# First FFN chunks of a decoder layer by rows of blocks, with h taken from PSUM and filler products in front

## The chip, the core and the metric

The kernel runs on one core of a Trainium2 chip. The core has TensorE (PE: matrix products and transposes, results in PSUM), VectorE (DVE), ScalarE (ACT), GpSimd (POOL), and SyncE (SP), which issues nearly all the loads. The metric is the device time of one execution in microseconds (us).

## What is computed

One layer of a hybrid decoder, 512 tokens of width 1024, all in f32:

```python
h = rms_norm(x, ffn1_norm)
x = x + 0.5 * (silu(h @ w_gate) * (h @ w_up)) @ w_down     # D_FF = 2816
# then: pooling and sliding-window attention with w_in and w_out,
# a second FFN of the same form, and x + sigmoid(rms_norm(x) @ w_g) * (p @ w_p)
```

The change touches only the beginning: loading x and the first weights, turning x so that features lie on partitions, multiplying it by the gains, and the first products of the first FFN.

## The kernel before

**Precision.** Each f32 operand is split into a high part in fp32r (written by ScalarE as a rounding copy) and a low part, the remainder (VectorE for activations, POOL for weights). A product is then three products of TensorE: high x high, low x high, high x low (`product`, lines 1112 to 1116). Weights come in chunks of 128 x 1024 f32 (512 KB) into a ring of four slots: `raw` (as loaded), `w_hi`, `w_lo`. For gate and up, one chunk is one block of 128 output features over all eight blocks k of input features, in the order gate 0, up 0, gate 1, up 1, and so on. `w_hi_done`, `w_ready` (low part done) and `w_used` (products done) count chunks.

**The norm.** h is not divided by the root of the mean square before the products. `h_hi` and `h_lo` are x times the gain; the statistic is made beside the products: ScalarE squares x block by block (`h_square`), VectorE adds the squares into `sumsq` (`h_add`), and one product with a tile of ones, `stat`, sums over the partitions. `rstd_of` on ScalarE makes the inverse root by Ln and Exp. VectorE applies it to the products' results.

**The opening.** SP loads x in four parts of 256 columns, in turn with the first four chunks, then p and eleven small gain vectors. PE turns x block by block into banks 4 to 7 (`turn_x`, four transposes a block). VectorE copies each to `x_t`; ScalarE makes `h_hi` from `x_t`, VectorE `h_lo`. PE multiplies pair by pair of blocks k, for the first two chunks (slots 0 and 1) into banks 0 and 1. Then it turns the gains and p, and does slots 2 and 3 in one go, with `stat` in the middle of slot 2. Each engine's order is written out by hand, with semaphores as the only link; an engine never passes over a waiting instruction.

**The loop.** `ffn_tensor` then goes through the chunks in groups of four, eight blocks each. It waits for the chunk's `w_ready` and for VectorE to have read the bank. On ScalarE `ffn_scalar` comes after `rstd_of(0, 4)`: its first action is the split of chunk 4 (line 468), which waits for the load and for slot 0 to be used. POOL's `lo_of` follows it. The load of chunk 4 itself waits on SP until slot 0's low part is made (`put`).

## Time and profile before

| | us |
|---|---|
| median of 3 runs | 938.45 |
| lowest, highest | 937.75, 938.58 |
| profiled execution | 938.35 |
| its span, first to last instruction | 936.6 |
| PE busy | 923.4 (99%) |
| PE weight loads busy | 759.6 (81%) |
| DVE, ACT, POOL busy | 297.9, 385.3, 414.0 |

A row of the order of time gives start, duration, engine, line of the kernel, operation, what it writes and reads, how many instructions are merged, and in brackets how long the engine had been idle and what ended that. Products overlap: a product's duration is longer than the distance to the next one's start, so paces are read from starts.

### The profile page before, as it was taken

The numbers are of one execution on the slowest core, as the hardware profiler recorded it, in microseconds if no ns is written. First come the engines' busy times: TensorE is split into PE (matmuls) and PEld (weight loads), VectorE is DVE, ScalarE is ACT, GpSimd is POOL, SyncE is SP. The second block draws the span as 40 slices with busy tenths as digits, with TensorE's granted clock in tenths as the row PEclk, the third lists the DMA queues.
The fourth block names the chain that finished last, engine by engine and source line by source line (L and its number), as shares of the span: only waits on it lengthen the run. The fifth ranks groups of instructions, "written<-read, shape, count | busy, mean of one in ns | idle before, by whom it ended". The sixth has DMA issues, their size and how long they took to land.

```text
span 936.6 us, 11393 instructions
## 1 busy us (share of the span) xinstructions
PE 923.4 (99%) x4104; PEld 759.6 (81%) x4104; DVE 297.9 (32%) x467; ACT 385.3 (41%) x514; POOL 414.0 (44%) x191
## 2 busy tenths in 40 slices
PE   7999999999999999999999999999999999999998
PEld 5888888888888888777788788888888888888886
DVE  6511122211100501659978532111112200410532
ACT  5734444433321421565844644433444321321641
POOL 3554444444444444345645354444444444444340
PEclk9999999999999999999999999999999999999999
DMA  8333333332332333231223143333333323332221
GB/s 251 108 113 99 102 90 94 108 90 90 107 95 90 90 112 90 60 99 34 68 68 113 54 126 103 99 90 94 107 90 91 108 93 90 99 103 90 74 73 56
DMA packets 129650, 89.25 MB, mean 95 GB/s; under 512 B 11312, under 2 KB 114776, under 8 KB 129624
## 3 DMA queue, kind: packets, MB, share of 16 engines
q1 hardware_dynamic: 129608, 88.90, 31.9%
q8 instruction: 16, 0.26, 0.1%
q14 instruction: 10, 0.08, 0.0%
q10 hardware_dynamic: 16, 0.00, 0.0%
HBM read 86.80 MB, written 2.10 MB: 95 GB/s over the span
## 4 chain that ended last, share of the span: by engine, by line
PE 94%; DVE 4%; issue 1%; DMA 0%; ACT 0%; DVEq 0%; ACTq 0%
PE bank L1114 31%; PE bank L1115 31%; PE bank L1116 31%; PE bank L1129 1%; DVE sumsq L745 1%; DVE h_lo L736 1%; DVE probs L923 1%; PE bank L1260 0%; DMA x_nat<-in_x 0%; PE bank L1134 0%; DVE x_t L1088 0%; DVE tmp L1087 0%; DVE pr_lo L949 0%; DVE small L931 0%; ACT h_hi L428 0%
## 5 line engine op out<-in xcount | busy, mean ns | idle before, releaser
L324 POOL TENSOR_TENSOR w_lo<-raw,w_hi 128x1024 fp32r<-128x1024 f32 x161 | 390.2, 2426 | 479.1 <-ACT w_hi L468 240.4
L1114 PE MATMUL bank<-h_hi,w_hi 128*128 128x512 f32 x848 | 335.2, 395 | 0.3 <-DVE h_lo L736 0.3
L1115 PE MATMUL bank<-h_lo,w_hi 128*128 128x512 f32 x848 | 330.7, 390 | 0.0
L1116 PE MATMUL bank<-h_hi,w_lo 128*128 128x512 f32 x848 | 330.6, 390 | 0.0
L1114 PEld LDWEIGHTS bank<-h_hi,w_hi 128*128 128x128 f32 x848 | 159.6, 188 | 36.8 <-issue 2.3
L1115 PEld LDWEIGHTS bank<-h_lo,w_hi 128*128 128x128 f32 x848 | 159.7, 188 | 34.5 <-issue 1.9
L1116 PEld LDWEIGHTS bank<-h_hi,w_lo 128*128 128x128 f32 x848 | 159.6, 188 | 33.2
L419 ACT ACTIVATE w_hi<-raw 128x1024 fp32r<-128x1024 f32 x81 | 85.7, 1060 | 223.3 <-PE bank L1116 218.6
L468 ACT ACTIVATE w_hi<-raw 128x1024 fp32r<-128x1024 f32 x80 | 84.4, 1060 | 190.9 <-PE bank L1116 190.9
L1114 PE MATMUL bank<-act_hi,w_hi 128*128 (+1 forms) x352 | 136.9, 389 | 0.0
L1115 PE MATMUL bank<-act_lo,w_hi 128*128 (+1 forms) x352 | 136.9, 389 | 0.0
L1116 PE MATMUL bank<-act_hi,w_lo 128*128 (+1 forms) x352 | 136.9, 389 | 0.0
L762 DVE TENSOR_TENSOR tmp<-bank,tmp 128x512 f32<-128x512 f32 x44 | 30.4, 692 | 285.9 <-ACT tmp L456 285.9
L1116 PEld LDWEIGHTS bank<-act_hi,w_lo 128*128 128x128 f32 x352 | 66.1, 188 | 13.8
L1114 PEld LDWEIGHTS bank<-act_hi,w_hi 128*128 128x128 f32 x352 | 66.1, 188 | 13.7
L1115 PEld LDWEIGHTS bank<-act_lo,w_hi 128*128 128x128 f32 x352 | 66.1, 188 | 13.6
L785 DVE SCALAR_TENSOR_TENSOR tmp<-bank,rstd 128x512 f32<-128x512 f32 x16 | 11.1, 692 | 197.1 <-PE bank L1116 196.7
L764 DVE TENSOR_TENSOR act_lo<-tmp,act_hi 128x512 f32 (+1 forms) x44 | 38.2, 869 | 39.5 <-ACT act_hi L458 39.5
L458 ACT ACTIVATE act_hi<-tmp 128x512 f32 (+1 forms) x44 | 27.8, 633 | 37.4 <-DVE tmp L762 37.4
L759 DVE TENSOR_TENSOR tmp<-bank,rstd 128x512 f32<-128x512 f32 x44 | 30.4, 690 | 36.7 <-PE bank L1116 30.7
L456 ACT ACTIVATE tmp<-tmp 128x512 f32<-128x512 f32 x44 | 27.4, 623 | 0.2
L736 DVE SCALAR_TENSOR_TENSOR h_lo<-x_t,gain,h_hi 128x512 fp32r<-128x512 f32 x32 | 26.2, 856 | 3.0 <-ACT h_hi L428 2.7
(149 smaller groups left out, 621.5 us busy)
## 6 DMA issues: line engine op xcount, KB each, us to landing
raw<-in_ffn_w_gate SPq DMA_DIRECT2D x44, 512.0 KB, 3.7
raw<-in_ffn_w_up SPq DMA_DIRECT2D x44, 512.0 KB, 3.7
raw<-in_ffn_w_down SPq DMA_DIRECT2D x44, 512.0 KB, 3.7
raw<-in_w_ple_gate SPq DMA_DIRECT2D x8, 512.0 KB, 3.7
raw<-in_w_in SPq DMA_DIRECT2D x6, 512.0 KB, 3.7
x_nat<-in_x SPq DMA_DIRECT2D x4, 512.0 KB, 7.0
raw<-in_w_in SPq DMA_DIRECT2D x8, 256.0 KB, 3.2
raw<-in_w_out SPq DMA_DIRECT2D x4, 512.0 KB, 3.4
```

What stands on the lines that cost most here:

```text
L324: pool.tensor_tensor(w_lo[:, slot, :], raw[:, slot, :], f32(w_hi[:, slot, :]), ALU.subtract).then_inc(w_ready, 1)
L419: nc.scalar.activation(w_hi[:, slot, :], raw[:, slot, :], ACT.Copy).then_inc(w_hi_done, 1)
L456: nc.scalar.activation(tmp[:, 2 * (f % 2), :], tmp[:, 2 * (f % 2), :], ACT.Silu).then_inc(silu_done, 1)
L458: nc.scalar.activation(act_hi[:, f + 2 * quad, :], tmp[:, 2 * (f % 2) + 1, :], ACT.Copy).then_inc(act_hi_done, 1)
L468: nc.scalar.activation(w_hi[:, slot, :], raw[:, slot, :], ACT.Copy).then_inc(w_hi_done, 1)
L736: nc.vector.scalar_tensor_tensor(h_lo[:, d, :], x_t[:, d, :], gain[:, ph * KD + d:ph * KD + d + 1], f32(h_hi[:, d, :]), ALU.mult, ALU.subt ...
L759: nc.vector.tensor_tensor(a, gb[:], rstd[:], ALU.mult).then_inc(gate_scaled, 1)
L762: nc.vector.tensor_tensor(t, ub[:], a, ALU.mult).then_inc(act_made, 1)
L764: nc.vector.tensor_tensor(act_lo[:, f + 2 * quad, :], t, f32(act_hi[:, f + 2 * quad, :]), ALU.subtract).then_inc(act_ready, 1)
L1114: nc.tensor.matmul(dst, a_hi, b_hi, start=first, stop=False)
L1115: nc.tensor.matmul(dst, a_hi, b_lo, start=False, stop=False)
L1116: return nc.tensor.matmul(dst, a_lo, b_hi, start=False, stop=last)
```

## The change

- **Loads.** x comes in five parts (blocks 0, 1, 2-3, 4-5, 6-7, from the list `FIRST`). Behind each part come the same rows of blocks of all four first chunks: for each block k one load of gate and one of up, each filling two slots.
- **Splits.** ScalarE's splits and POOL's low parts of the first four chunks go by the same parts, over all four slots at once. VectorE makes the low part of row 0 itself.
- **h from PSUM.** ScalarE's rounding and VectorE's remainder read the turned x from PSUM, in banks 4 to 6 in turn; the copy to `x_t` comes after them.
- **Products.** For each block k PE does all four slots (12 products), with turns of x in between. Blocks 6 and 7 come last, slot by slot, after the turns of gains and p; `stat` stands behind slot 0's last rows.
- **Filler.** Seven products of the tile of ones with itself into bank 3, which nobody reads, stand ahead of the first turns. The turn of the first gains moves ahead of those of x.
- The loads' counts for later chunks are shifted to fit, and `w_ready` of the first four chunks now rises by four at once, with the last part.

```diff
@@ -50,11 +50,13 @@
     CHUNKS = PLE + KD
     TWO_PART = {C_Q, C_Q + 1, C_Q + 2, C_Q3} | {C_WA + i for i in range(HALF)}
     QUADS = NF // 2
+    WARM = 7
+    FIRST = ((0, 1), (1, 2), (2, 4), (4, 6), (6, 8))
 
     def loads_of(slot, c0, quad=0):
 
         extra = sum(1 for c in TWO_PART if c <= c0 and c % SLOTS == slot)
-        return 16 * (c0 // SLOTS + 1 + extra) + 16 * quad
+        return 16 * (c0 // SLOTS + extra) + 16 * quad
 
     es = ExitStack()
     with es:
...
@@ -230,19 +234,26 @@
 
 
             x_v = x[0].rearrange("(b p) c -> p b c", p=P)
-            W = D // 4
-
-            def load_x(i):
-                sp.dma_start(x_nat[:, :, i * W:(i + 1) * W], x_v[:, :, i * W:(i + 1) * W]).then_inc(x_loaded[i], 16)
-
-            load_x(0)
-            gate_up(0, ffn1_w_gate, 0)
-            load_x(1)
-            gate_up(1, ffn1_w_up, 0)
-            load_x(2)
-            load_x(3)
-            gate_up(2, ffn1_w_gate, 1)
-            gate_up(3, ffn1_w_up, 1)
+            def load_x(eng, s):
+                k0, k1 = FIRST[s]
+                eng.dma_start(x_nat[:, :, k0 * P:k1 * P], x_v[:, :, k0 * P:k1 * P]).then_inc(x_loaded[s], 16)
+
+            def load_first(s):
+
+                k0, k1 = FIRST[s]
+                for j, w in enumerate((ffn1_w_gate, ffn1_w_up)):
+                    for k in range(k0, k1):
+                        sp.dma_start(raw[:, j:SLOTS:2, k * P:(k + 1) * P],
+                                     w[0, k * P:(k + 1) * P, 0:2 * P].rearrange("p (f c) -> p f c", f=2))\
+                            .then_inc(first_loaded[s], 16)
+
+            load_x(sp, 0)
+            load_first(0)
+            load_x(sp, 1)
+            load_first(1)
+            for s in range(2, len(FIRST)):
+                load_x(sp, s)
+                load_first(s)
             sp.dma_start(p_nat[:], p[0, 0].rearrange("(b p) c -> p b c", p=P)).then_inc(p_loaded, 16)
 
             rows = KD
@@ -324,8 +335,17 @@
                 pool.tensor_tensor(w_lo[:, slot, :], raw[:, slot, :], f32(w_hi[:, slot, :]),
                                    ALU.subtract).then_inc(w_ready, 1)
 
-            for c in range(SLOTS):
-                lo_of(c, c + 1)
+            for s in range(1, len(FIRST)):
+                cols = slice(FIRST[s][0] * P, FIRST[s][1] * P)
+                if s < len(FIRST) - 1:
+                    pool.wait_ge(first_hi_done, s + 1)
+                else:
+                    pool.wait_ge(w_hi_done, SLOTS)
+                ins = pool.tensor_tensor(w_lo[:, :, cols], raw[:, :, cols], f32(w_hi[:, :, cols]), ALU.subtract)
+                if s < len(FIRST) - 1:
+                    ins.then_inc(first_lo_done, 1)
+                else:
+                    ins.then_inc(w_ready, SLOTS)
             with pool.Fori(1, (C_K + 2) // SLOTS) as quad:
                 for slot in range(SLOTS):
                     lo_of(slot, quad * SLOTS + slot + 1)
...
@@ -492,30 +512,46 @@
 
             act.dma_start(gain_nat[0:KD, :], ffn1_norm[0].rearrange("(k p) -> k p", p=P)).then_inc(gain1_loaded, 16)
 
-            split(0)
+            def first_split(s):
+                cols = slice(FIRST[s][0] * P, FIRST[s][1] * P)
+                act.wait_ge(first_loaded[s], 32 * (FIRST[s][1] - FIRST[s][0]))
+                ins = nc.scalar.activation(w_hi[:, :, cols], raw[:, :, cols], ACT.Copy)
+                if s < len(FIRST) - 1:
+                    ins.then_inc(first_hi_done, 1)
+                else:
+                    ins.then_inc(w_hi_done, SLOTS)
+
+            def first_round(d):
+                act.wait_ge(x_turned, d + 1)
+                nc.scalar.activation(h_hi[:, d, :], bank[4 + d % 3][:], ACT.Copy,
+                                     scale=gain[:, d:d + 1]).then_inc(h_hi_done, 1)
+
+            first_split(0)
             act.wait_ge(gain1_ready, 1)
-            h_round(0, 0)
-            h_round(0, 1)
-            split(1)
+            first_round(0)
+            first_split(1)
+            first_round(1)
             h_square(0, 0)
+            first_split(2)
+            first_round(2)
             h_square(0, 1)
-            h_round(0, 2)
-            h_round(0, 3)
+            first_split(3)
+            first_round(3)
             h_square(0, 2)
+            first_split(4)
+            first_round(4)
             h_square(0, 3)
-            h_round(0, 4)
-            h_round(0, 5)
-            split(2)
-            h_round(0, 6)
-            h_round(0, 7)
-            split(3)
-            for d in range(HALF, KD):
-                h_square(0, d)
+            first_round(5)
+            h_square(0, 4)
+            first_round(6)
+            h_square(0, 5)
+            first_round(7)
+            h_square(0, 6)
+            h_square(0, 7)
             for k in range(2):
                 act.wait_ge(p_turned, k + 1)
-                nc.scalar.activation(pt_hi[:, k, :], bank[5 + k][:], ACT.Copy).then_inc(p_hi_done, 1)
-            rstd_of(0, 4)
-            act.wait_ge(gain_ready, 3)
+                nc.scalar.activation(pt_hi[:, k, :], bank[6 - 2 * k][:], ACT.Copy).then_inc(p_hi_done, 1)
+            rstd_of(0, 5)
             ffn_scalar(0, FFN1)
             for d in range(HALF, KD):
                 h_square(1, d)
@@ -819,25 +855,47 @@
                                       sink_in[:].rearrange("p (g t) -> p g t", g=2)).then_inc(gain_ready, 1)
 
 
-            for pair in range(HALF):
-                for d in (2 * pair, 2 * pair + 1):
-                    dve.wait_ge(x_turned, d + 1)
-                    nc.vector.tensor_copy(x_t[:, d, :], bank[4 + d % 4][:]).then_inc(x_ready, 1)
-                dve.wait_ge(x_ready, 2 * pair + 2)
-                if pair == 0:
-                    dve.wait_ge(gain_turned, 1)
-                    nc.vector.tensor_copy(gain[:, 0:KD], bank[7][:, 0:KD]).then_inc(gain1_ready, 1)
-                    dve.wait_ge(gain1_ready, 1)
-                h_rest(0, 2 * pair)
-                h_rest(0, 2 * pair + 1)
-                if pair == 1:
-                    h_add(0, 1)
-            for d in range(2, KD):
-                h_add(0, d)
+            def first_rest(d):
+                dve.wait_ge(h_hi_done, d + 1)
+                nc.vector.scalar_tensor_tensor(h_lo[:, d, :], bank[4 + d % 3][:], gain[:, d:d + 1],
+                                               f32(h_hi[:, d, :]), ALU.mult, ALU.subtract).then_inc(h_ready, 1)
+
+            def first_copy(d):
+                nc.vector.tensor_copy(x_t[:, d, :], bank[4 + d % 3][:]).then_inc(x_ready, 1)
+
+            dve.wait_ge(gain_turned, 1)
+            nc.vector.tensor_copy(gain[:, 0:KD], bank[7][:, 0:KD]).then_inc(gain1_ready, 1)
+            dve.wait_ge(gain1_ready, 1)
+            first_rest(0)
+            dve.wait_ge(first_hi_done, 1)
+            nc.vector.tensor_tensor(w_lo[:, :, 0:P], raw[:, :, 0:P], f32(w_hi[:, :, 0:P]),
+                                    ALU.subtract).then_inc(first_lo_dve, 1)
+            first_copy(0)
+            first_rest(1)
+            first_copy(1)
+            first_rest(2)
+            first_copy(2)
+            h_add(0, 1)
+            first_rest(3)
+            first_copy(3)
+            h_add(0, 2)
+            first_rest(4)
+            first_copy(4)
+            h_add(0, 3)
+            first_rest(5)
+            first_copy(5)
+            h_add(0, 4)
+            first_rest(6)
+            first_copy(6)
+            h_add(0, 5)
+            first_rest(7)
+            first_copy(7)
+            h_add(0, 6)
+            h_add(0, 7)
             later_gains()
             for k in range(2):
                 dve.wait_ge(p_hi_done, k + 1)
-                nc.vector.tensor_tensor(pt_lo[:, k, :], bank[5 + k][:], f32(pt_hi[:, k, :]), ALU.subtract)\
+                nc.vector.tensor_tensor(pt_lo[:, k, :], bank[6 - 2 * k][:], f32(pt_hi[:, k, :]), ALU.subtract)\
                     .then_inc(p_ready, 1)
             dve.wait_ge(gain_ready, 3)
             ffn_vector(0, FFN1)
...
@@ -1197,49 +1255,64 @@
 
             def turn_x(d):
 
-                if d % 2 == 0:
-                    pe.wait_ge(x_loaded[d // 2], 16)
-                if d == 3:
-                    pe.wait_ge(gain1_ready, 1)
-                if d >= 4:
-                    pe.wait_ge(x_ready, d - 3)
+                for s in range(len(FIRST)):
+                    if d == FIRST[s][0]:
+                        pe.wait_ge(x_loaded[s], 16)
+                if d >= 3:
+                    pe.wait_ge(x_ready, d - 2)
                 for b in range(NB):
-                    ins = turn(bank[4 + d % 4][:, b * P:(b + 1) * P], x_nat[:, b, d * P:(d + 1) * P])
+                    ins = turn(bank[4 + d % 3][:, b * P:(b + 1) * P], x_nat[:, b, d * P:(d + 1) * P])
                 ins.then_inc(x_turned, 1)
 
+            def first_ready(k):
+
+                pe.wait_ge(h_ready, k + 1)
+                if k == 0:
+                    pe.wait_ge(first_lo_dve, 1)
+                elif k < FIRST[4][0]:
+                    pe.wait_ge(first_lo_done, 1 if k < 2 else k // 2 + 1)
+                else:
+                    pe.wait_ge(w_ready, SLOTS)
+
+            def first_step(k):
+                first_ready(k)
+                for j in range(SLOTS):
+                    from_h(bank[j][:], j, k, k + 1)
+
+            pe.wait_ge(dve_consts, 1)
+            for i in range(WARM):
+                nc.tensor.matmul(bank[3][:, 0:P], ones[:], ones[:], start=True, stop=True)
+            pe.wait_ge(gain1_loaded, 16)
+            turn(bank[7][:, 0:KD], gain_nat[0:KD, :], KD).then_inc(gain_turned, 1)
             turn_x(0)
             turn_x(1)
-            pe.wait_ge(gain1_loaded, 16)
-            turn(bank[7][:, 0:KD], gain_nat[0:KD, :], KD).then_inc(gain_turned, 1)
+            first_step(0)
             turn_x(2)
+            first_step(1)
             turn_x(3)
-
-            for pair in range(HALF):
-                pe.wait_ge(h_ready, 2 * pair + 2)
-                for j in range(2):
-                    if pair == 0:
-                        pe.wait_ge(w_ready, j + 1)
-                    ins = from_h(bank[j][:], j, 2 * pair, 2 * pair + 2)
-                    if pair == HALF - 1:
-                        ins.then_inc(w_used, 1)
-                if pair < 2:
-                    turn_x(4 + 2 * pair)
-                    turn_x(5 + 2 * pair)
+            first_step(2)
+            turn_x(4)
+            first_step(3)
+            turn_x(5)
+            turn_x(6)
+            first_step(4)
+            turn_x(7)
+            first_step(5)
             pe.wait_ge(gains_loaded, 16 * 11)
-            pe.wait_ge(x_ready, KD)
             turn(bank[7][:, 0:GAINS], gain_nat[:], GAINS).then_inc(gain_turned, 1)
             pe.wait_ge(p_loaded, 16)
             for k in range(2):
+                pe.wait_ge(x_ready, KD - 2 + k)
                 for b in range(NB):
-                    ins = turn(bank[5 + k][:, b * P:(b + 1) * P], p_nat[:, b, k * P:(k + 1) * P])
+                    ins = turn(bank[6 - 2 * k][:, b * P:(b + 1) * P], p_nat[:, b, k * P:(k + 1) * P])
                 ins.then_inc(p_turned, 1)
-            for j in range(2, SLOTS):
-                pe.wait_ge(w_ready, j + 1)
-                from_h(bank[j][:], j, 0, HALF)
-                if j == 2:
+            first_ready(KD - 2)
+            first_ready(KD - 1)
+            for j in range(SLOTS):
+                from_h(bank[j][:], j, KD - 2, KD).then_inc(w_used, 1)
+                if j == 0:
                     pe.wait_ge(dve_consts, 4 + PAD)
-                    stat(0, 4)
-                from_h(bank[j][:], j, HALF, KD).then_inc(w_used, 1)
+                    stat(0, 5)
             ffn_tensor(0, FFN1)
 
 
```

## Rows read from the trace of the kernel before

**Rows 1.** The page: busy time of each engine; the slices of PE.

```profile
PE 923.4 (99%) x4104; PEld 759.6 (81%) x4104; DVE 297.9 (32%) x467; ACT 385.3 (41%) x514; POOL 414.0 (44%) x191
...
PE   7999999999999999999999999999999999999998
```

**Rows 2.** Order of time to 15 us: start, duration, engine, line, operation, idle before.

```profile
1.19 0.29 POOL L319 TENSOR_SCALAR_AFFINE_SELECT ident<-ident 128x128 f32<-128x128 f32 x1 [0.24 <-POOL ident L317]
...
4.31 1.94 PE L1129 MATMUL bank<-ident,x_nat 128*128 128x128 f32 x8 [4.31 <-DMA x_nat<-in_x]
5.51 1.47 DVE L825 COPY x_t<-bank 128x512 f32<-128x512 f32 x2 [3.57 <-PE bank L1129]
5.92 1.06 ACT L419 ACTIVATE w_hi<-raw 128x1024 fp32r<-128x1024 f32 x1 [3.23 <-DMA raw<-in_ffn_w_gate]
...
7.21 1.34 ACT L428 ACTIVATE h_hi<-x_t,gain 128x512 fp32r<-128x512 f32 x2 [0.24 <-DVE gain L829]
8.04 2.58 DVE L736 SCALAR_TENSOR_TENSOR h_lo<-x_t,gain,h_hi 128x512 fp32r<-128x512 f32 x2 [0.86 <-ACT h_hi L428]
...
14.55 0.68 DVE L745 TENSOR_TENSOR sumsq<-sumsq,tmp 128x512 f32<-128x512 f32 x1
```

**Rows 3.** Order of time on PE, 10 to 15 us: the first products.

```profile
10.67 0.79 PE L1114 MATMUL bank<-h_hi,w_hi 128*128 128x512 f32 x1 [0.29 <-DVE h_lo L736]
...
11.69 0.63 PE L1116 MATMUL bank<-h_hi,w_lo 128*128 128x512 f32 x1
12.12 0.63 PE L1114 MATMUL bank<-h_hi,w_hi 128*128 128x512 f32 x1
...
14.43 0.39 PE L1116 MATMUL bank<-h_hi,w_lo 128*128 128x512 f32 x1
14.65 0.39 PE L1114 MATMUL bank<-h_hi,w_hi 128*128 128x512 f32 x1
```

**Rows 4.** Busy time by stretch; last three columns: granted clock, DMA share, GB/s.

```profile
12.00:14.00 2.00, 2.00 (x5) 1.18 (x5) 1.30 (x2) 1.73 (x3) 1.41 (x1) 1.00 1.15 338
...
16.00:18.00 2.00, 2.00 (x12) 1.72 (x11) 1.73 (x3) 1.29 (x3) 0.00 (x0) 1.00 0.07 21
```

**Rows 5.** Order of time on PE: products on either side of transposes.

```profile
15.12 0.40 PE L1116 MATMUL bank<-h_hi,w_lo 128*128 128x512 f32 x1
...
16.46 0.40 PE L1115 MATMUL bank<-h_lo,w_hi 128*128 128x512 f32 x1
...
25.38 0.39 PE L1116 MATMUL bank<-h_hi,w_lo 128*128 128x512 f32 x1
...
27.05 0.39 PE L1115 MATMUL bank<-h_lo,w_hi 128*128 128x512 f32 x1
```

**Rows 6.** Order of time, 29 to 39 us, PE, ACT, POOL: statistic to loop.

```profile
29.57 1.02 PE L1134 MATMUL bank<-sumsq,ones 128*128 128x512 f32 x2
...
38.63 0.39 PE L1114 MATMUL bank<-h_hi,w_hi 128*128 128x512 f32 x1
...
30.70 0.69 ACT L444 ACTIVATE rstd<-bank,scalars 128x512 f32<-128x512 f32 x1
31.40 1.28 ACT L446 ACT_TABLE_LOAD   x1
33.35 1.28 ACT L468 ACT_TABLE_LOAD   x1
34.64 2.01 ACT L468 ACTIVATE w_hi<-raw 128x1024 fp32r<-128x1024 f32 x2
...
35.78 4.76 POOL L324 TENSOR_TENSOR w_lo<-raw,w_hi 128x1024 fp32r<-128x1024 f32 x2 [10.24 <-ACT w_hi L468]
```

**Rows 7.** Order of time on PE and POOL around FFN2's statistic.

```profile
526.48 1.12 PE L1134 MATMUL bank<-sumsq,ones 128*128 128x512 f32 x2 [0.81 <-DVE sumsq L745]
...
531.45 4.77 POOL L324 TENSOR_TENSOR w_lo<-raw,w_hi 128x1024 fp32r<-128x1024 f32 x2 [15.56 <-ACT w_hi L468]
```

**Rows 8.** The chain that ended last, at the statistic: start, us, what.

```profile
29.73 0.86 PE bank L1134 x2
```

More of the change, by code:

```diff
@@ L123, in layer @@
         bank = [es.enter_context(nc.psum_tensor(f"bank{i}", [P, S], F32)) for i in range(8)]
-        x_loaded = [sem(f"x_loaded{i}") for i in range(4)]
+        x_loaded = [sem(f"x_loaded{i}") for i in range(len(FIRST))]
+        first_loaded = [sem(f"first_loaded{i}") for i in range(len(FIRST))]
+        first_hi_done, first_lo_dve, first_lo_done = sem("first_hi_done"), sem("first_lo_dve"), sem("first_lo_done")
         p_loaded, gains_loaded, sinks_loaded = sem("p_loaded"), sem("gains_loaded"), sem("sinks_loaded")
```

## The prediction

> **What bounds the kernel now.** I read the page first. TensorE (PE) is busy for 923.4 of the 936.6 us of span [rows 1], so the time is PE's work plus the 13 us in which it has none, and an edit pays only where it changes those 13 us or the pace of the products. Then I read the order of time of the first 40 us, since the diff touches nothing behind them. PE starts at 4.31 with transposes of x, its first product starts at 10.67, and the first product of the loop over FFN chunks (chunk 4) at 38.63 [rows 2, 3, 6]. From there PE goes on without a gap, one product each 0.2275 us. So the change is worth what it moves the start at 38.63, and nothing else counts. I call that start the loop start. The 96 products of the opening cost 96 x 0.2275 = 21.8 us of the 38.63, whatever their order.
>
> The third thing to see is the pace: until about 14 us products start 0.43 us apart (11.69 to 12.12), later 0.22 apart (14.43 to 14.65) [rows 3]. That is the lower and the upper of PE's two levels, 1.2 and 2.4 GHz, although the granted clock in the row of that stretch reads 1.00 [rows 4]; here only the pitch tells the level. Eight products ran at the lower one, which cost 8 x 0.2 = 1.6 us.
>
> The fourth is what runs up to the loop start. The opening's statistic (ones times the sum of squares) starts on PE at 29.57. ScalarE then has in a row: Ln at 30.70, a table load at 31.40, Exp, a table load at 33.35, and only then the two splits at 34.64, the first of which is chunk 4; POOL makes its low part from 35.78, two in 4.76 us, so chunk 4 is ready at 38.16 [rows 6]. From statistic to ready chunk: 8.6 us. PE covers this with 36 products (8.2 us) and the statistic itself (0.86), 9.06 us, and arrives 0.45 us after the chunk. A wait of nearly nine microseconds is hidden with half a microsecond to spare. FFN2 has the same chain with one table load less: statistic at 526.48, POOL from 531.45, ready at 533.84, 7.4 us = 8.6 less 1.28 [rows 7]. So I trust 8.6.
>
> **The change, part by part.**
>
> *The first product.* The seven filler products can start when the identity is made (1.19 + 0.29 = 1.48, POOL) [rows 2]; an f32 product of 512 columns takes 0.86 at the upper level [rows 8], so one of 128 columns 0.215, or 0.43 at the lower: 7 x 0.43 = 3.0, and PE is free at 4.55. That is 0.25 later than its start on x now. The turn of the gains takes 0.2, so x's first block starts at 4.75. VectorE saw the first turned block 1.20 after its start (5.51 against 4.31), and from ScalarE's rounding to VectorE's remainder it was 0.83 (7.21 to 8.04) [rows 2]: rounding at 5.95, first_rest at 6.8. The copy to x_t no longer stands in between; that is what "straight from PSUM" saves. first_rest takes 0.7 (the add at 14.55 took 0.68 with POOL idle) to 1.3 (two remainders in 2.58 beside POOL); take 0.75. Then VectorE makes w_lo of row 0, 0.7 to 1.3, its first part before POOL has its own work. First product at 8.5, between 8.2 and 9.1, against 10.67: 2.2 us earlier. The loads don't set it: the gate load of 512 KB, which has the 512 KB of x ahead of it, let ScalarE start at 5.92, and in the new order x's first block and its weights are 512 KB together, so they are there by about 4.5.
>
> *From there to the statistic.* Now 60 products and 16 transposes of x lie between the first product and the statistic; then 78 products and 24 transposes. 78 x 0.2275 = 17.75. Eight transposes between products cost 1.34 - 2 x 0.2275 = 0.885 (15.12 to 16.46) and the turns of gains and p 1.67 - 0.455 = 1.215 (25.38 to 27.05) [rows 5], so 3 x 0.885 + 1.215 = 3.9. Sum 21.6. The same sum for the kernel now (10.67 + 13.65 + 1.77 + 1.215 + 1.6 for the low clock = 28.9) is 0.66 short of 29.57, some of it a wait for the second chunk's low part; I carry 0.3, since row blocks are ready sooner. The statistic starts at 8.5 + 21.6 + 0.3 = 30.4, which is 0.8 *later* than now: it now stands behind 78 products instead of 60.
>
> *Is PE fed in between?* One row of blocks is 12 products and a turn, 2.73 + 0.44 = 3.2 us. VectorE needs for it a remainder, a copy (two in 1.47) and an add (0.68), 2.1 us, and up to 3 beside POOL [rows 2]; ScalarE a rounding, a square and half a split of 1.06, 1.8; POOL 1.2. The loads run at 338 GB/s until after 14 us and are over in 16 to 18 [rows 4], so all 4 MB of x and first weights are there at about 14, and the last split and its low part by about 20, while the last two rows are wanted at 29. The tightest are row 2's low part (13.5 against 14.9) and the last add (29.4 against 30.4). I cost these at nothing; if the cover goes, VectorE's last two adds put up to 1 us before the statistic. SP issues 16 weight loads in place of four, about 0.5 us each, in time while the engines are saturated. The reload of all four slots now waits for the last low part (20) instead of slot by slot (17.5); it takes 4 us and is wanted at 33: nothing.
>
> *From the statistic to the loop.* This part of ScalarE's order is untouched: rstd, then the split of chunk 4. But the statistic now stands behind slot 0's last rows, and only slots 1 to 3's last rows, 18 products (4.1 us), follow it. PE is through at 30.4 + 0.86 + 4.1 = 35.4 and chunk 4 is ready at 30.4 + 8.6 = 39.0, plus 0.05. So PE stands idle for 3.7 us in front of the loop, a wait that doesn't exist now. What follows is covered: the next chunk comes 2.4 us later and PE works 5.4 us on each. Loop start at 39.05 against 38.63: 0.4 us later. The 3.3 us by which PE is through earlier, 38.63 to 35.4, go into the wait.
>
> *The clock.* No row shows what the filler does to the level. From below: it is at the upper level by the first product, and nothing is to be added. From above: it is no better than now, eight products at the lower, 1.6 us. PE is then busy from 1.55 to 6.3 almost without a break, where it now is for 4.31 to 6.3; I lean to the lower end and take 0.4. The Trainium skill, "TensorE: Matmul & The Clock Gate", section "What's actually happening", says that the idle array is the throttled one and that sustained work releases it; the rows agree, the pitch halves after dense products.
>
> Sum: 38.63 becomes 39.05 + 0.4 = 39.45, +0.8 us. The profiled execution took 938.35 with a span of 936.6, the runs' median is 938.45. 938.35 + 0.8 = 939.2.
>
> **The rivals.**
>
> 1. *The clock falls in the new idle time.* PE has no gap of this length once it runs, so no row shows what follows one. What the start shows is the price of the lower level: some eight products, 1.6 us. 939.2 + 1.6 = 940.8, slower than before. It decides once the wait for chunk 4 is long enough for the level to drop. For it: 3.7 us without work is over four times the gap in rows 7. Against it: the gap of 0.81 in front of FFN2's statistic [rows 7] cost nothing behind it. The same page of the Trainium skill, section "Why this matters for your kernels", warns that a long idle gap between bursts takes the array back to half rate; that rule speaks for this rival, and no run shown bears on it. Chance 0.14.
> 2. *The filler does not raise the clock.* Then the lower level lasts as now until 12 to 14 us, from 8.5 on: up to 13 products x 0.2 = 2.6 in place of 0.4, about 941.0. For it: the transposes of 4.31 to 6.3 and 8.41 to 10 did not raise it. Against: the filler more than doubles the unbroken stretch. Chance 0.12.
> 3. *The wait for chunk 4 does not come about.* If its split did not stand behind rstd, the loop would start at 35.4 and the time would be 935.1. Against it is the whole chain in rows 6 and 7. Chance 0.04.
> 4. *The filler works at once.* The level is up by the first turns, those take half, the first product comes at 8.0, the statistic at 29.7, the loop at 38.3: 938.0. Chance 0.08.
> 5. *Small loads are slow.* 21 issues in place of eight, each with its own start and end. The second kind of weights waits for row 4 only from 21 us on, so it decides only if the stream takes over 5 us longer; then about 942. The Trainium skill, "DMA: Bandwidth & Descriptors", section "Rules for kernel authors", speaks against the change in wanting few, large transfers; by it the loads run longer, which the slack above would take up. Chance 0.04.
>
> **How the numbers follow.** Forecast as summed 0.58, the rivals 0.14, 0.12, 0.04, 0.08, 0.04. A measurement of this kernel can tell about 0.2%, 1.9 us, from no change: 936.6 to 940.3. Faster is rival 3: 0.04. Slower are rivals 1, 2 and 5, less their mild ends, 0.26. Within is the forecast and rival 4 with those ends: 0.70. The range leaves out rival 3 and the worst of 1, 2 and 5: 937.5 to 941.3.
>
> **What would show it.** First product near 8.5; turns of x interleaved with groups of 12 products; the statistic near 30.4; PE idle for 3.7 us with the release "POOL w_lo" in front of the loop's first product, at about 39; the same three table loads. If PE's idle time there is under 2 us, my chain is wrong. If products behind the gap start 0.43 apart, rival 1 is right; if those up to 12 us do, rival 2. If VectorE's sumsq releases the statistic, the adds were not covered.

## The result

The changed kernel takes 943.0 us, median of 6 runs (941.56 to 943.19), against 938.56 for the kernel before: ratio 1.0043, 95% interval 1.0033 to 1.0054. It is slower by 4.4 us, 0.4%. The forecast was 939.2 with a range up to 941.3; the time lies outside it, and on the side that I gave 0.26.

| | before | after |
|---|---|---|
| profiled execution, its span | 938.35, 936.6 | 943.06, 941.3 |
| first product | 10.67 | 8.53 |
| products at the lower level at the start | 8 | 12 |
| statistic | 29.57 | 33.11 |
| PE idle in front of the loop | 0 | 3.48 |
| loop start | 38.63 | 41.72 |
| products at the lower level behind it | 0 | 7 to 8 |

Order of time on PE in the kernel after, the same view as [rows 2, 3].

```profile
1.53 3.36 PE L1284 MATMUL bank<-ones 128*128 128x128 f32 x14 [1.53 <-DVE head_ones L838]
4.82 0.27 PE L1187 MATMUL bank<-ident,gain_nat 8*128 8x8 f32 x1
5.02 1.11 PE L1187 MATMUL bank<-ident,x_nat 128*128 128x128 f32 x4
6.45 1.11 PE L1187 MATMUL bank<-ident,x_nat 128*128 128x128 f32 x4 [0.31 <-DMA x_nat<-in_x]
8.53 0.77 PE L1172 MATMUL bank<-h_hi,w_hi 128*128 128x512 f32 x1 [0.97 <-DVE w_lo L871]
...
13.36 0.63 PE L1174 MATMUL bank<-h_hi,w_lo 128*128 128x512 f32 x1
13.79 0.87 PE L1187 MATMUL bank<-ident,x_nat 128*128 128x128 f32 x4
14.41 0.47 PE L1172 MATMUL bank<-h_hi,w_hi 128*128 128x512 f32 x1
14.72 0.39 PE L1173 MATMUL bank<-h_lo,w_hi 128*128 128x512 f32 x1
```

The filler runs, the first product comes 2.1 us earlier than before, and the 12 products of row 0 take from 8.53 to 13.79, 5.26 us; at the upper level they would take 2.73. In this execution the filler had not raised the level when the first product came.

From the statistic to the loop, first PE, then ScalarE and POOL, the same view as [rows 6].

```profile
33.11 1.02 PE L1192 MATMUL bank<-sumsq,ones 128*128 128x512 f32 x2
...
37.86 0.39 PE L1174 MATMUL bank<-h_hi,w_lo 128*128 128x512 f32 x1
41.72 0.79 PE L1172 MATMUL bank<-h_hi,w_hi 128*128 128x512 f32 x1 [3.48 <-POOL w_lo L335]
42.31 0.63 PE L1173 MATMUL bank<-h_lo,w_hi 128*128 128x512 f32 x1
42.74 0.63 PE L1174 MATMUL bank<-h_hi,w_lo 128*128 128x512 f32 x1
...
34.16 0.69 ACT L464 ACTIVATE rstd<-bank,scalars 128x512 f32<-128x512 f32 x1 [0.30 <-PE bank L1192]
34.87 1.28 ACT L466 ACT_TABLE_LOAD   x1
...
36.82 1.28 ACT L488 ACT_TABLE_LOAD   x1
38.11 2.00 ACT L488 ACTIVATE w_hi<-raw 128x1024 fp32r<-128x1024 f32 x2
...
39.24 4.67 POOL L335 TENSOR_TENSOR w_lo<-raw,w_hi 128x1024 fp32r<-128x1024 f32 x2 [16.43 <-ACT w_hi L488]
```

Statistic at 33.11, chunk 4 ready at 39.24 + 2.34 = 41.58: 8.5 us, as forecast. PE is through at 38.1 and stands still until POOL releases it. Behind the gap products start 0.43 apart. Busy time by stretch of the kernel after (granted clock, DMA share and GB/s last) now shows the lower level itself: 0.50.

```profile
38.00:40.00 2.00, 0.25 (x2) 0.00 (x0) 0.00 (x0) 1.99 (x3) 0.76 (x1) 1.00 0.00 0
40.00:42.00 2.00, 0.28 (x1) 0.28 (x2) 0.00 (x0) 1.97 (x3) 2.00 (x2) 0.91 0.00 0
42.00:44.00 2.00, 2.00 (x5) 1.54 (x6) 1.05 (x2) 1.08 (x3) 1.92 (x1) 0.50 0.42 120
44.00:46.00 2.00, 2.00 (x8) 1.62 (x7) 1.06 (x2) 2.00 (x3) 1.37 (x1) 0.74 0.82 237
```

The account closes: the loop starts 3.1 us later (41.72 against 38.63), and eight products then take 3.47 us (41.72 to 45.19) in place of 1.82, 1.65 more. Together 4.7, which is the difference of the spans.

### The profile page after: what moved, and what is told of

Read it like the earlier page. It is cut to its first block, busy times and chain, and to the rows that moved or that the text cites. A ratio compares the mean times of both kernels' runs of the same rounds, so it can differ in the third digit from the quotient of the medians.

```text
span 941.3 us, 11441 instructions
## 1 busy us (share of the span) xinstructions
PE 928.3 (99%) x4118; PEld 763.9 (81%) x4118; DVE 294.0 (31%) x468; ACT 385.4 (41%) x515; POOL 413.0 (44%) x191
## 4 chain that ended last, share of the span: by engine, by line
PE 92%; DVE 4%; issue 3%; ACT 1%; DMA 0%; POOL 0%; SPq 0%; DVEq 0%; POOLq 0%; ACTq 0%
PE bank L1172 30%; PE bank L1174 30%; PE bank L1173 30%; PE bank L1187 1%; DVE sumsq L781 1%; DVE probs L981 1%; PE bank L1333 0%; DMA raw<-in_ffn_w_up 0%; DVE x_t L1146 0%; DVE tmp L1145 0%; DVE pr_lo L1007 0%; POOL w_lo L335 0%; DVE h_lo L772 0%; DVE small L989 0%; PE bank L1192 0%
## 5 line engine op out<-in xcount | busy, mean ns | idle before, releaser
L335 POOL TENSOR_TENSOR w_lo<-raw,w_hi 128x1024 fp32r<-128x1024 f32 x157 | 380.1, 2424 | 472.6 <-ACT w_hi L488 248.0
L439 ACT ACTIVATE w_hi<-raw 128x1024 fp32r<-128x1024 f32 x77 | 81.5, 1061 | 218.7 <-PE bank L1174 218.6
L488 ACT ACTIVATE w_hi<-raw 128x1024 fp32r<-128x1024 f32 x80 | 84.4, 1060 | 192.2 <-PE bank L1174 192.0
L798 DVE TENSOR_TENSOR tmp<-bank,tmp 128x512 f32<-128x512 f32 x44 | 30.4, 692 | 287.6 <-ACT tmp L476 287.6
L1172 PEld LDWEIGHTS bank<-act_hi,w_hi 128*128 128x128 f32 x352 | 66.1, 188 | 13.8
L800 DVE TENSOR_TENSOR act_lo<-tmp,act_hi 128x512 f32 (+1 forms) x44 | 38.1, 866 | 39.5 <-ACT act_hi L478 39.5
L795 DVE TENSOR_TENSOR tmp<-bank,rstd 128x512 f32<-128x512 f32 x44 | 30.4, 690 | 37.4 <-PE bank L1174 33.9
```

The lines of the kernel that those rows point to most:

```text
L335: pool.tensor_tensor(w_lo[:, slot, :], raw[:, slot, :], f32(w_hi[:, slot, :]), ALU.subtract).then_inc(w_ready, 1)
L439: nc.scalar.activation(w_hi[:, slot, :], raw[:, slot, :], ACT.Copy).then_inc(w_hi_done, 1)
L488: nc.scalar.activation(w_hi[:, slot, :], raw[:, slot, :], ACT.Copy).then_inc(w_hi_done, 1)
L795: nc.vector.tensor_tensor(a, gb[:], rstd[:], ALU.mult).then_inc(gate_scaled, 1)
L798: nc.vector.tensor_tensor(t, ub[:], a, ALU.mult).then_inc(act_made, 1)
L800: nc.vector.tensor_tensor(act_lo[:, f + 2 * quad, :], t, f32(act_hi[:, f + 2 * quad, :]), ALU.subtract).then_inc(act_ready, 1)
```

## The experiments

Two questions: is the wait in front of the loop, with the fall of the clock behind it, one separable cost with one cause (the statistic's place)? And why did the filler bring nothing: is it useless for the level, or is its effect lost before the first product? All times are medians beside the kernel before on the same chip, whose medians were 938.7 to 938.8.

| run | median (lowest to highest) | ratio to before, 95% |
|---|---|---|
| e1_no_filler | 943.36 (943.13 to 943.72) | 1.0049 (1.0035 to 1.0063) |
| e2_filler16 | 945.28 (944.84 to 945.95) | 1.0069 (1.0055 to 1.0083) |
| e3_no_wait | 936.33 (935.21 to 937.97) | 0.9974 (0.9963 to 0.9984) |
| e4_gap_filled | 941.16 (939.05 to 941.85) | 1.0024 (1.0015 to 1.0033) |
| e5_tables_only | 941.86 (937.58 to 942.06) | 1.0019 (1.0008 to 1.0031) |
| e6_no_wait_no_filler | 937.15 (936.52 to 937.82) | 0.9980 (0.9971 to 0.9989) |
| e7_no_wait_holes | 935.17 (935.01 to 935.74) | 0.9960 (0.9947 to 0.9974) |
| e8_late_stat | 944.55 (944.35 to 946.07) | 1.0063 (1.0051 to 1.0076) |
| e9_round_first | 935.21 (934.95 to 935.43) | 0.9963 (0.9950 to 0.9977) |
| e10_before_filled | 938.06 (937.62 to 940.41) | 0.9997 (0.9988 to 1.0006) |
| e11_after_holes | 940.38 (939.04 to 940.63) | 1.0014 (1.0005 to 1.0023) |

### The wait: e8_late_stat, e3_no_wait, e4_gap_filled, e5_tables_only

**e8_late_stat**, the kernel before with the statistic moved:

```diff
-                from_h(bank[j][:], j, 0, HALF)
-                if j == 2:
+                from_h(bank[j][:], j, 0, 2)
+                if j == 3:
                     pe.wait_ge(dve_consts, 4 + PAD)
                     stat(0, 4)
-                from_h(bank[j][:], j, HALF, KD).then_inc(w_used, 1)
+                from_h(bank[j][:], j, 2, KD).then_inc(w_used, 1)
```

> The kernel before, with nothing changed but the place of the statistic: six products into slot 3, so that 18 products stand between it and the loop in place of 36. Theory A (the wait in front of the loop comes from this place alone): PE gets to the statistic 18 products (4.1 us) later, chunk 4 is ready 8.6 us after it, a gap of 3.6 us opens in front of the loop and the level falls behind it: 938.6 + 3.6 + 1.5 to 3.0, 943.7 to 945.2. Rival F (the wait of the changed kernel comes from the loads by rows or from all four slots being freed together): no gap here, 938.6.

Measured 944.55, as theory A put it. The first products of e8's loop on PE:

```profile
42.97 0.79 PE L1114 MATMUL bank<-h_hi,w_hi 128*128 128x512 f32 x1 [3.49 <-POOL w_lo L324]
43.56 0.63 PE L1115 MATMUL bank<-h_lo,w_hi 128*128 128x512 f32 x1
```

The kernel before has no loads by rows, no shared release of slots and no filler, and gets the same gap (3.49 against 3.48 us) with slow products behind it, from one moved instruction. The place of the statistic is enough to cause both. Of the 6.0 us by which e8's profiled execution is longer than that of the kernel before, 3.5 are the gap and 1.7 the slow products; most of the rest is a statistic 0.7 us later than the move alone makes it, behind a first product at 11.10 in place of 10.67 and products at the lower level until 15.6.

**e3_no_wait**, the changed kernel with ScalarE's order mended; the loop's first round of splits is written out and the loop begins at 2:

```diff
+            act.preload_act_table_set("natural_log_exp_and_others")
             first_split(0)
...
+            split(SLOTS)
             rstd_of(0, 5)
             ffn_scalar(0, FFN1)
```

> The changed kernel with ScalarE's order mended: the split of chunk 4 stands ahead of the inverse root (the loop's first round of splits is written out for this), and the table that holds copy, square, Ln and Exp is loaded at the start, so no load stands between. Chunk 4 is then ready 3.6 us after the statistic begins and PE arrives after 5.0. Theory A (the wait costs 3.5 us and the drop of the level behind it 1.5 us, nothing else): PE goes into the loop without a gap at 38.1, at 0.23 us pitch, and the time is 943.0 - 3.6 - 1.5 = 937.9. Rival B (something else bounds that place, the read of bank 0 or the loads): a gap of over 1 us stays and the time is 940 or more.

Measured 936.33. ScalarE of e3, where the split of chunk 4 stands first and no table load is left before it or between Ln and Exp:

```profile
31.89 1.06 ACT L439 ACTIVATE w_hi<-raw 128x1024 fp32r<-128x1024 f32 x1 [0.81 <-PE bank L1182]
32.85 0.67 ACT L464 ACTIVATE rstd<-bank,scalars 128x512 f32<-128x512 f32 x1
33.55 0.63 ACT L466 ACTIVATE rstd<-rstd 128x512 f32<-128x512 f32 x1
```

PE goes into the loop without a gap. The same opening is now 2.4 us faster than before instead of 4.4 slower. It gained 6.7, 1.6 more than forecast: in its profiled execution the level also rose earlier at the start (at 11.4 in place of 13.8), which is the matter of the next section. e4, whose code up to the loop is that of the changed kernel, had an earlier rise as well (12.2), so it comes without e3's edit; what sets it in an execution stays open.

**e4_gap_filled**, fifteen unread products of h between the statistic's tail and the loop:

```diff
+            pe.wait_ge(gain_ready, 1)
+            for i in range(15):
+                nc.tensor.matmul(bank[7][:], h_hi[:, 0, 0:P], h_hi[:, 0, :], start=True, stop=True)
             ffn_tensor(0, FFN1)
```

> The changed kernel with fifteen unread products of h (512 columns, 0.2275 us each, 3.4 us) in PE's idle time in front of the loop. The wait for chunk 4 stays as it is. Theory A (the 3.5 us without work let the level fall, which cost seven products x 0.2 us): the loop starts at the same 41.7 us, but at 0.23 us pitch at once, and the time falls by 1.5 us to 941.5. Rival B (the level fell for another reason, or falls by chance): the first seven products of the loop stay 0.43 us apart and the time stays at 943.

Measured 941.16. The wait is kept, only PE is busy in it, and the loop starts at the upper level:

```profile
40.59 0.49 PE L1172 MATMUL bank<-h_hi,w_hi 128*128 128x512 f32 x1
40.92 0.39 PE L1173 MATMUL bank<-h_lo,w_hi 128*128 128x512 f32 x1
```

So the fall comes from the idle time. Its price, read from the eight slow products of the changed kernel, is some 1.6 us. The median is lower by 1.8; the profiled execution also had the earlier rise at the start, so the median alone does not give the price.

**e5_tables_only**, of e3 the line with the table alone.

> The changed kernel with one line added: ScalarE loads the table that holds copy, square, Ln and Exp at the start, so the two loads of 1.28 us between the statistic and the split of chunk 4 go; their order stays. Theory A (the wait is the chain's length less PE's cover, and the level falls only behind a long idle time): chunk 4 is ready 6.0 us after the statistic begins, PE waits 1.1 us in place of 3.5 and goes on at 0.23 us pitch; time 936.3 (no wait at all) + 1.1 = 937.4. Rival C (any wait in front of the loop drops the level): 1.1 us of wait and seven or more products 0.43 apart, 939 to 940.

Measured 941.86, far off both the 937.4 and most of the gain. Two things were wrong in my expectation. First, only the load before Exp went; the one at the loop's entry stayed (35.76 in ScalarE's row below), so the wait is 2.20 us and not 1.1. Second, the level fell here too, but late: the first five products behind the gap ran fast, those from 42.0 on slow. e5 on ScalarE, on PE, and by stretch:

```profile
35.76 1.28 ACT L488 ACT_TABLE_LOAD   x1
...
40.68 0.49 PE L1173 MATMUL bank<-h_hi,w_hi 128*128 128x512 f32 x1 [2.20 <-POOL w_lo L335]
41.01 0.39 PE L1174 MATMUL bank<-h_lo,w_hi 128*128 128x512 f32 x1
...
41.99 0.63 PE L1175 MATMUL bank<-h_hi,w_lo 128*128 128x512 f32 x1
42.41 0.63 PE L1173 MATMUL bank<-h_hi,w_hi 128*128 128x512 f32 x1
42.84 0.63 PE L1174 MATMUL bank<-h_lo,w_hi 128*128 128x512 f32 x1
```

```profile
42.00:44.00 2.00, 2.00 (x6) 1.63 (x5) 1.41 (x2) 2.00 (x3) 1.30 (x2) 0.50 0.90 256
```

Two of its twelve runs took 937.6, 4.3 below the median. That would fit executions in which neither the start nor the gap met the lower level (some 12 + 8 products x 0.2 us), but only one execution has a trace, so this stays open.

### The filler: e1, e2, e6, e7, e11, e10, e9

**e1_no_filler** sets `WARM = 0`, **e2_filler16** `WARM = 16`.

> The changed kernel without its seven filler products. Theory A (the filler never reached the clock: in the changed kernel products run 0.43 us apart until 13.8, as long as before): the level rises at about the same time, 14 us; the first block of x is turned at 4.3 in place of 5.0, the first product comes up to 0.6 us earlier, at 8.0, and the time falls by 0 to 0.5 us from 943.0. Rival B (the filler did its part and without it the level would rise later still): the rise moves from 14 to 15 or later and the time rises by 0.5 to 1.5 us.

> Sixteen filler products in place of seven, so PE is busy without a break from 1.5 to about 9.2 us (16 x 2 x 0.24 = 7.7). Theory A (this kind of filler, f32 over 128 columns, does not raise the level at all): first product at about 12.7 to 13, at the lower level, the level rises 3 to 5 us after it, time 943 + 4 = 947. Rival B (the filler was only too short): the fillers' own pitch halves before 9 us, the first product comes at 10 to 11 at 0.23 us pitch, and the time is 943 + 2.5 - 2.6, about 943, or less.

e1 took 943.36, 0.4 more than with the filler: neither theory, and no clear difference, since the intervals of the two ratios overlap (1.0035 to 1.0063 against 1.0033 to 1.0054). In its trace the level rises at 12.9, earlier than in the kernel after, and the statistic starts at 32.42, 0.7 us earlier. What it gains there it loses behind the loop's gap, where 13 products run slow (41.04 to 46.75) in place of 8. e2 took 945.28, between its two theories, and its trace says why. PE of e2, then by stretch:

```profile
1.54 5.52 PE L1284 MATMUL bank<-ones 128*128 128x128 f32 x32 [1.54 <-DVE head_ones L838]
...
11.14 0.47 PE L1172 MATMUL bank<-h_hi,w_hi 128*128 128x512 f32 x1 [2.91 <-DVE w_lo L871]
11.45 0.40 PE L1173 MATMUL bank<-h_lo,w_hi 128*128 128x512 f32 x1
11.68 0.41 PE L1174 MATMUL bank<-h_hi,w_lo 128*128 128x512 f32 x1
11.91 0.61 PE L1172 MATMUL bank<-h_hi,w_hi 128*128 128x512 f32 x1
12.32 0.63 PE L1173 MATMUL bank<-h_lo,w_hi 128*128 128x512 f32 x1
```

```profile
12.00:14.00 2.00, 2.00 (x6) 1.54 (x5) 0.85 (x2) 1.21 (x2) 0.72 (x1) 0.50 1.10 360
```

The 32 filler instructions take 5.5 us, where 14 take 3.36, 0.24 each: the level rose within them. Then PE idles 2.91 us for the first product's operands. The first three products run at the upper level, and then it falls, after the gap as in e5, and stays low until 15.3. The filler raises the level; the hole behind it takes the effect away. Of the 2.9 us by which this execution is longer than that of the kernel after, 1.5 are a later loop start (43.25) and the rest is 14 slow products behind the same gap of 3.48 us. e4, whose code up to here is the changed kernel's, shows the same with seven: its second turn of x took 0.66 in place of 1.11, its first product was followed after 0.31 us, and then

```profile
8.46 0.49 PE L1172 MATMUL bank<-h_hi,w_hi 128*128 128x512 f32 x1 [1.32 <-DVE w_lo L871]
8.77 0.61 PE L1173 MATMUL bank<-h_lo,w_hi 128*128 128x512 f32 x1
9.18 0.63 PE L1174 MATMUL bank<-h_hi,w_lo 128*128 128x512 f32 x1
```

So with seven products the level rises in some executions by the first turns (e3, e4) and in others not until dense products (after, e5), and where it rises it does not last.

**e6_no_wait_no_filler** is e3 with `WARM = 0`: what the seven are worth where no wait follows.

> As e3_no_wait, without the seven filler products. Theory D (the filler raises the level before 5 us, the 2 to 3 us without products before the first real one take most of it back, and what is left is an earlier second rise: at 11.3 us in e3_no_wait against 12.9 in e1_no_filler): time 936.3 + 0.5 to 0.8, about 937. Rival A (the filler is worth nothing): 936.3 within 0.3. If it is worth what one would hope of it (twelve products at the upper level), 939.

Measured 937.15, 0.8 us over e3: the time that theory D gave, though the intervals of the two ratios overlap. Its mechanism, a second rise that comes earlier with the filler, is not seen: in the profiled execution of e6 the level rises at 11.6, in that of e3 at 11.4. So what seven fillers are worth with the holes behind them is 0.8 us at most, and by which way is not shown.

**e7_no_wait_holes** adds to e3 fillers in PE's two holes:

```diff
             turn_x(0)
+            fill(3)
             turn_x(1)
+            fill(6)
             first_step(0)
```

> As e3_no_wait, with nine more filler products: three between the turns of x's first two blocks and six behind them, where PE idles for 0.9 and 1.4 us before the first product. Theory D (the level falls in those holes): it stays up, the first twelve products start 0.23 us apart, first product at about 8.5 as now, and the time falls by 7 x 0.2 = 1.4 us to 934.9. Rival E (fillers don't hold the level, only 512-column products do): products slow until 11 as now, 936.3, or up to 0.8 worse if the fillers run over into the first product.

Measured 935.17, within 0.7 us from lowest to highest, where e3 spread over 2.8. e7 on PE:

```profile
5.94 1.43 PE L1297 MATMUL bank<-ones 128*128 128x128 f32 x6
7.20 0.60 PE L1195 MATMUL bank<-ident,x_nat 128*128 128x128 f32 x4
7.64 1.50 PE L1297 MATMUL bank<-ones 128*128 128x128 f32 x12
8.90 0.48 PE L1180 MATMUL bank<-h_hi,w_hi 128*128 128x512 f32 x1
9.21 0.40 PE L1181 MATMUL bank<-h_lo,w_hi 128*128 128x512 f32 x1
9.45 0.39 PE L1182 MATMUL bank<-h_hi,w_lo 128*128 128x512 f32 x1
```

All twelve products of row 0 run at 0.23 us. Without a hole the level stays, and the ten runs of e7 and e9 lie within 0.8 us. e7 and e9 are the fastest kernels of the study, 0.4% under the kernel before.

**e11_after_holes** puts the same nine into the changed kernel and keeps its wait.

> The changed kernel with the nine more filler products of e7_no_wait_holes, and its wait for chunk 4 kept. Theory A and D (costs add up: slow first products and the wait with its drop are separate): the first twelve products run at the upper level, 943.0 - 2.4 = 940.6, between 940.2 and 941.8, with the gap of 3.5 us and slow products behind it as before. Rival J (the level is worth nothing while the wait follows): 943.0.

Measured 940.38 (forecast 940.6): 2.6 us of the changed kernel's 943.0 were the slow start. The gap of 3.48 us and some eight slow products are still there, and from here to e7 it is 5.2 us, the wait's 3.5 and the fall's 1.7. Its runs spread over 1.6 us in spite of the fillers; the number of slow products behind the gap differs between the kept traces (8 to 14), which may be the reason, but only one execution of e11 has a trace.

**e10_before_filled**, the kernel before with six, six and three fillers in its holes, tests how much the filler alone would have brought.

> The kernel before, with nothing but fifteen filler products in PE's holes: six ahead of the first turns, six behind the turn of the gains (hole from 6.4 to 8.4 us), three ahead of the first product. Theory D (fillers work if they leave no hole): the eight slow products and part of the slow transposes go at the upper level, 938.8 - 1.6 = 937.2. It says how much of the gain of e7_no_wait_holes is the filler's (then 1.6 of 3.6 us) and how much the order by rows and the earlier h bring. Rival I (the filler's gain is tied to the changed order): 938.8.

Measured 938.06, where theory D gave 937.2; ratio 0.9997 with 1 inside the interval: not separable from nothing. Its products are fast from the first, but VectorE and POOL have them wait. e10 on VectorE and PE:

```profile
8.10 2.77 DVE L736 SCALAR_TENSOR_TENSOR h_lo<-x_t,gain,h_hi 128x512 fp32r<-128x512 f32 x2 [0.87 <-ACT h_hi L428]
...
10.93 0.50 PE L1114 MATMUL bank<-h_hi,w_hi 128*128 128x512 f32 x1 [0.97 <-DVE h_lo L736]
...
13.26 0.50 PE L1114 MATMUL bank<-h_hi,w_hi 128*128 128x512 f32 x1 [0.68 <-POOL w_lo L324]
```

In the old order PE at the upper level runs into the low part of the second chunk and stands 0.68 us, and its first product comes 0.26 later than in the kernel before. The order by rows, which feeds PE with 12 products a row, has no such wait in e7. That this is what lets the level pay is argued from the two traces; no run isolates it. The level stayed up behind both gaps here, of 0.97 and 0.68 us.

**e9_round_first** is e7 with `first_round(0)` ahead of `first_split(0)`.

> As e7_no_wait_holes, with ScalarE's first rounding of h ahead of its first split. In e3_no_wait the split begins at 5.59, when the up weights have landed, and the rounding, whose input is turned at about 5.7, stands behind it until 6.1. Theory G (the first product waits for split, rounding, remainder and low part in a row): rounding and remainder now run beside the wait for the weights, the first product comes 0.3 to 0.5 us earlier, 935.17 - 0.4 = 934.8. Rival H (the low part of row 0, which needs the split, becomes the last): the split ends 0.5 us later, the gain is nil, 935.2.

Measured 935.21, no gain. ScalarE's rounding in e7, then in e9:

```profile
6.25 0.69 ACT L532 ACTIVATE h_hi<-bank,gain 128x512 fp32r<-128x512 f32 x1 [0.16 <-PE bank L1195]
6.18 0.69 ACT L532 ACTIVATE h_hi<-bank,gain 128x512 fp32r<-128x512 f32 x1 [3.51 <-PE bank L1195]
```

In both it began when x was turned, so in e7 it had not waited for the split: theory G fails for these executions, and the chain into the first product is turn, rounding, remainder, low part. It is not refuted for all. In both, the first turn ran at the lower level (1.11 and 1.06 us). In e3 it took 0.65, from 4.85, and there the rounding did start right behind the split, at 6.12; whether the edit would pay in such an execution stays open.

## Why the prediction was wrong

**Right, with its sizes.** The first product (8.5 forecast, 8.53 measured; the filler was released by VectorE's constants at 1.53 and not by the identity, at nearly the same time). The chain from statistic to chunk 4 (8.6, 8.5). The idle time in front of the loop (3.7, 3.48), its release by POOL's low part, and that nothing else takes its place. That a statistic behind 78 products comes later and eats all of PE's earlier start. PE was fed throughout: no idle entry on PE between 8.53 and 38.

Two steps failed, and both are the clock's: the term for the start was too small, and the fall behind the wait was put at nothing in the sum.

**Wrong in size: the clock at the start.** I took 0.4 us between bounds of 0 and 1.6, leaning on an unbroken busy stretch of 4.7 us. It was 2.5 us (12 products in 5.26). That is nearly all of what moved the statistic from 30.4 to 33.1. My upper bound was itself short, since it counted only the eight slow products of the kernel before; an earlier first product has more products to run until the level rises, which it did at about 14 us in the profiled executions of both kernels (in others between 11.4 and 15.6, with the filler and without). The text gives this price in rival 2 (up to 13 products, 2.6 us), and the term in the sum should have had it. That rival's own sum is wrong as well: 939.2 less 0.4 plus 2.6 is 941.4, not 941.0, and lies outside the range. What I had not asked was whether the level survives the hole between filler and first product: e2 shows that it does not, e7 what it is worth if there is none.

**Wrong in the cases: two rivals at once.** I gave the fall behind the wait 0.14 and the useless filler 0.12 and treated them as exclusive, each stated with a time below 941.3; the sum itself has nothing for the fall. Neither excludes the other, and their prices add (e11 and e7 take them off one by one): 939.2 - 0.4 + 2.6 + 1.6 = 943.0, which is the measured time. That it fits to the tenth is partly luck: 1.6 was the price of eight slow products at the start of the kernel before, and behind the same gap e1 had 13 and e2 14. The forecast's own 3.7 us of idle PE was the condition of rival 1, so its chance should have been high as soon as I believed the wait. I held against it a gap of 0.81 us [rows 7], which says nothing of one four times as long. The Trainium skill, "TensorE: Matmul & The Clock Gate", section "Why this matters for your kernels", warns that a long idle gap between bursts takes the array back to half rate, and the trace agrees: 0.50 granted from 42 to 44 us.

**Loads.** The first weights landed at 5.6, not 4.5. In the profiled execution this cost nothing, since x was turned only at 6.1 and the rounding began at 6.24. Between 10 and 16 us the loads moved 347 to 367 GB/s, as much as the large ones [rows 4]; but between 2 and 8 us they moved 230 to 281, where the kernel before had 316 to 336. The Trainium skill, "DMA: Bandwidth & Descriptors", section "Rules for kernel authors", wants few, large transfers; the trace agrees with that in the first 8 us and not later. No run separates the size of the loads from their order.

**Where the expected gain went.** Against the kernel before, e7 is 3.5 us faster, and this includes that e7 no longer pays the slow start of the kernel before, some 1.6 us. The changed kernel pays 5.2 for the wait and the fall, and 2.6 for its own slow start: -3.5 + 5.2 + 2.6 = 4.3, measured 4.4. The three terms are steps between measured kernels and must add up; the evidence is that the two last steps came out near their forecasts (940.4 for 940.6, 935.2 for 934.9).

## What to carry to other kernels

When products are pulled forward, look at what was hidden behind their tail: here a chain of 8.6 us on three engines had 0.45 us to spare, and moving one statistic 18 products nearer to its consumer cost 3.5 us plus the clock. Filler products brought 2.6 us where they filled PE's time up to the first real product (e11), at most 0.8 where holes of about a microsecond followed (e6 against e3), and nothing measurable where other engines then held PE back (e10); look at the release of the first real product, and fill up to it. Rivals that don't exclude each other have to be added up before the range is set.

## What the runs showed of the hardware

- After an idle time PE can start at the upper level and fall a little later: in e5 it ran five products after a gap of 2.20 us, in e2 three after 2.91 us.
- Eight to fourteen products ran slow behind the loop's gap (after and e5: 8, e11: 9, e1: 13, e2: 14), which cost 1.5 to 2.9 us.
- The granted clock reads 1.00 in the first stretches although the products' pitch is that of the lower level; from the first rise on it agreed with the pitch where both were read (0.50 at 42 to 44 us in the kernel after, 0.50 at 8 to 10 us in e3).
- The table load at the loop's entry stayed although the table that holds copy, square, Ln and Exp had been loaded at the start (e5, 35.76).
- VectorE's low part of row 0 took 1.63 us in e2, where POOL's subtraction ran beside it (9.18 to 10.44), against 0.68 in e3, where POOL began only after it.
